# Attention of a two-layer trunk: softplus from a bounded score, and sums over later keys by two f32r products each

## The reference, cut to what matters

```
z = einsum('bhqd,bhkd->bhqk', q, k)                 # q already scaled
visible = arange(nk) < start + arange(nq)           # strictly causal
log_keep = where(visible, log_sigmoid(-z), 0)       # = -softplus(z)
later = cumsum(log_keep, reverse over keys) - log_keep
w = where(visible, exp(log_sigmoid(z) + later), 0)
out = einsum('bhqk,bhkd->bhqd', w, v)
```

## Time and profile before

| | |
|---|---|
| median of three runs | 1333.18 us |
| the profiled execution, own time | 1332.71 us |
| its span | 1331.0 us |
| TensorE busy | 1285.5 us (97%) |
| VectorE busy | 808.4 us (61%) |
| ScalarE busy | 640.2 us (48%) |
| GpSimd busy | 328.2 us (25%) |

### The profile page before, as it was taken

The page is one execution under the profiler, slowest core; times in us unless marked ns, Lnnn a source line. Parts: engine busy times, 40 slices in busy tenths (PEclk is TensorE's granted clock), DMA queues, the critical chain, the costliest instruction groups (busy, mean ns, idle before and its releaser), DMA issues.

```text
span 1331.0 us, 23141 instructions
## 1 busy us (share of the span) xinstructions
PE 1285.5 (97%) x9758; PEld 1173.9 (88%) x9758; DVE 808.4 (61%) x1357; ACT 640.2 (48%) x989; POOL 328.2 (25%) x183
## 2 busy tenths in 40 slices
PE   7999998999999999999999999999999999999996
PEld 6999855999999999999998988877787898998984
DVE  6989654466667375483656456365557673745745
ACT  4344587455346245263564335364354462552634
POOL 0001154265110201102654124114652102011040
PEclk9999999999999999999999999999999999999997
DMA  6641100222233223223222112112322333232311
GB/s 190 150 101 34 66 1 1 83 77 85 76 94 118 77 92 122 77 93 123 65 68 67 59 63 65 64 64 95 95 64 95 96 104 101 92 116 95 99 60 64
DMA packets 112151, 111.49 MB, mean 84 GB/s; under 512 B 8144, under 2 KB 109728, under 8 KB 112048
## 3 DMA queue, kind: packets, MB, share of 16 engines
q1 hardware_dynamic: 108528, 106.77, 25.0%
q0 software_dynamic: 3120, 3.15, 1.5%
q10 hardware_dynamic: 400, 0.11, 0.0%
HBM read 107.91 MB, written 2.10 MB: 83 GB/s over the span
## 4 chain that ended last, share of the span: by engine, by line
PE 79%; DVE 9%; ACT 7%; issue 2%; DMA 2%; POOL 1%; DVEq 0%; SPq 0%; ACTq 0%
PE pb L827 41%; PE pb L1037 6%; PE pb L1039 6%; PE pb L1038 6%; PE pb L998 2%; PE pb L999 2%; PE pb L1000 2%; PE pb L839 1%; PE pb L938 1%; PE pb L939 1%; PE pb L937 1%; ACT wh L1502 1%; PE pb L1279 1%; DVE wl L2164 1%; PE pb L876 1%
## 5 line engine op out<-in xcount | busy, mean ns | idle before, releaser
L676 POOL TENSOR_TENSOR wl<-raw,wh 128x2048 fp32r<-128x2048 f32 x40 | 185.3, 4633 | 690.0 <-ACT wh L1502 690.0
L827 PE MATMUL pb<-hidh,wh 128*128 128x264 f32 (+1 forms) x744 | 197.4, 319 | 0.2 <-DVE wl L2164 0.2
L827 PE MATMUL pb<-hidl,wh 128*128 128x264 f32 (+1 forms) x744 | 197.4, 320 | 0.0
L827 PE MATMUL pb<-hidh,wl 128*128 128x264 f32 (+1 forms) x744 | 197.3, 319 | 0.0
L1502 ACT ACTIVATE wh<-raw 128x2048 fp32r<-128x2048 f32 x73 | 139.3, 1908 | 95.9 <-DMA raw<-in_mlp_w_down 61.0
L827 PE MATMUL pb<-hh,wh 128*128 128x264 f32 (+1 forms) x584 | 150.0, 318 | 4.9 <-DVE qd L2803 1.6
L827 PE MATMUL pb<-hl,wh 128*128 128x264 f32 (+1 forms) x584 | 145.0, 310 | 0.0
L827 PE MATMUL pb<-hh,wl 128*128 128x264 f32 (+1 forms) x584 | 145.0, 309 | 0.0
L827 PEld LDWEIGHTS pb<-hidh,wh 128*128 128x128 f32 x744 | 123.7, 188 | 10.3 <-DVE wl L2164 0.6
L827 PEld LDWEIGHTS pb<-hidh,wl 128*128 128x128 f32 x744 | 123.4, 188 | 9.7
L827 PEld LDWEIGHTS pb<-hidl,wh 128*128 128x128 f32 x744 | 123.4, 188 | 9.5
(11 more groups left out here) (476 smaller groups left out, 3259.6 us busy)
## 6 DMA issues: line engine op xcount, KB each, us to landing
raw<-in_mlp_w_up SPq DMA_DIRECT2D x32, 1024.0 KB, 5.3
raw<-in_mlp_w_down SPq DMA_DIRECT2D x32, 1024.0 KB, 5.1
raw<-in_w_in_c SPq DMA_DIRECT2D x16, 1024.0 KB, 5.3
raw<-in_w_in_ab SPq DMA_DIRECT2D x8, 1024.0 KB, 7.1
raw<-in_w_out_ab SPq DMA_DIRECT2D x4, 1024.0 KB, 5.1
raw<-in_w_out_c SPq DMA_DIRECT2D x4, 1024.0 KB, 5.1
wl<-in_w_in_ab POOLq DMA_DIRECT2D x3, 1024.0 KB, 11.6
x_tok<-in_x SPq DMA_DIRECT2D x2, 1024.0 KB, 8.3
```

What stands on the lines that cost most here:

```text
L676: pool.tensor_tensor(wl[:, c % RING, :], raw[:, c % RING, :], wh[:, c % RING, :].bitcast(F32), ALU.subtract).then_inc(w_lo, 1)
L827: mm = pe.matmul(pb[:, bank + b, 0:z_ - a], lhs, rhs[:, a:z_], start=first and hi and k == 0, stop=last and k == len(todo) - 1)
```

## The change

`z` is cut at `Z_MAX` = 60 by VectorE into `al` (`bound`), ScalarE takes Exp and Ln of it, without Abs, and VectorE takes max(z, ln(1 + exp(min(z, 60)))) (`soft`). ScalarE copies the result to f32r (`high_part`), VectorE subtracts (`split`). The sums over later keys are made from the two parts by f32r products (`sph`, `spl`) with f32r copies of `ntri` and `nones`; `later_a`, `later_b` and their buffers go, and each piece is multiplied on its own. `sp` shares its memory with `spl` and has eight rows, used by `sp_row`. On VectorE `bound(g+2)` stands between `soft(g)` and `split(g)`; on ScalarE `high_part(g)` stands behind `weigh(g-2)`. `softplus_0` and `acc0` stay as they were.

```
+Z_MAX = 60.0
...
         m0b = ExitStack()
-        sp = sb("sp", [P, 6, 512], F32, m0b)
+        al = sb("al", [P, 2, 512], F32, m0b)
+        w_att = sb("w_att", [P, 4, 512], F32, m0b)
         ntri = sb("ntri", [P, P], F32, m0b)
         nones = sb("nones", [P, P], F32, m0b)
         hide = sb("hide", [P, UNIT_A], F32, m0b)
@@ -240,12 +242,15 @@
         ident_r = sb("ident_r", [P, P], F32R, m0b)
         hide_r = sb("hide_r", [P, UNIT_A], F32R, m0b)
         hide0_r = sb("hide0_r", [P, 4 * NMETA], F32R, m0b)
-        al = sb("al", [P, 2, 512], F32, m0b)
+        ntri_r = sb("ntri_r", [P, P], F32R, m0b)
+        nones_r = sb("nones_r", [P, P], F32R, m0b)
         sp0 = sb("sp0", [P, 2, 4 * NMETA], F32, m0b)
         w0 = sb("w0", [P, 2, 4 * NMETA], F32, m0b)
-        lb = sb("lb", [P, 2, 144], F32, m0b)
-        lc = sb("lc", [P, 2, 272], F32, m0b)
-        w_att = sb("w_att", [P, 4, 512], F32, m0b)
+        sp_home = ExitStack()
+        sp = sb("sp", [P, 8, 512], F32, sp_home)
+        sp_home.close()
+        spl = sb("spl", [P, 8, 512], F32R, m0b)
+        sph = sb("sph", [P, 8, 512], F32R, m0b)
         m0b.close()
...
+        def sp_row(g):
+
+            return 6 + g % 2 if g % 6 < 2 and g // 6 % 2 else g % 6
...
             pe.wait_ge(att_consts, 10)
-            pe.wait_ge(mask_r, 3)
+            pe.wait_ge(mask_r, 5)
...
             def acc(g):
 
                 i, n, s, hd, ps = head(g)
-                sa, sb_ = sp[:, hd, :], sp[:, 2 + hd, :]
-                pe.wait_ge(sp_ready, g + 1)
-
-                def later(c0, c1, x_, stop):
-                    return pe.matmul(pb[:, ZB[n], c0:c1], nones[:, :], x_, start=False, stop=stop, skip_group_check=True)
-
-                pe.matmul(pb[:, ZB[n], 0:UNIT[s]], ntri[:, :], sp[:, n, 0:UNIT[s]], start=False, stop=False, skip_group_check=True)
+                a, b = sp_row(6 * i + hd), sp_row(6 * i + 2 + hd)
+                pe.wait_ge(sp_low, g + 1)
+
+                def later(c0, c1, row, x0, stop=False):
+                    for x_ in (sph, spl):
+                        mm = pe.matmul(pb[:, ZB[n], c0:c1], nones_r[:, :], x_[:, row, x0:x0 + c1 - c0], start=False,
+                                       stop=stop and x_ is spl, skip_group_check=True)
+                    return mm
+
+                for x_ in (sph, spl):
+                    pe.matmul(pb[:, ZB[n], 0:UNIT[s]], ntri_r[:, :], x_[:, sp_row(g), 0:UNIT[s]], start=False, stop=False,
+                              skip_group_check=True)
                 if s == 0:
-                    later(144, 160, sa[:, 0:16], False)
-                    later(416, 432, sa[:, 0:16], False)
-                    mm = later(288, 432, sa[:, 16:160], True)
+                    later(144, 160, a, 0)
+                    later(416, 432, a, 0)
+                    mm = later(288, 432, a, 16, True)
                 elif s == 1:
-                    later(128, 256, sa[:, 160:288], False)
-                    pe.wait_ge(later_ready, 4 * i + hd + 1)
-                    mm = later(256, 400, lb[:, hd, :], True)
+                    later(128, 256, a, 160)
+                    later(256, 400, a, 288)
+                    later(384, 400, a, 0)
+                    mm = later(256, 400, a, 16, True)
                 else:
-                    later(112, 240, sb_[:, 0:P], False)
-                    pe.wait_ge(later_ready, 4 * i + hd + 3)
-                    mm = later(240, 512, lc[:, hd, :], True)
+                    later(112, 240, b, 0)
+                    later(240, 512, b, 128)
+                    later(240, 368, a, 160)
+                    later(368, 512, a, 288)
+                    later(496, 512, a, 0)
+                    mm = later(368, 512, a, 16, True)
                 mm.then_inc(acc_ready, 1)
 
...
+            act.activation(ntri_r[:, :], ntri[:, :], ACT.Copy).then_inc(mask_r, 1)
+            act.activation(nones_r[:, :], nones[:, :], ACT.Copy).then_inc(mask_r, 1)
...
                 n = g % 6
                 c = UNIT[n // 2]
-                act.wait_ge(z_ready, g + 1)
-                if g >= 2:
-                    act.wait_ge(sp_ready, g - 1)
-                softplus_part(al[:, g % 2, 0:c], pb[:, ZB[n], 0:c]).then_inc(l_ready, 1)
+                a = al[:, g % 2, 0:c]
+                act.wait_ge(z_bounded, g + 1)
+                me.step(act.activation(a, a, ACT.Exp))
+                me.settle()
+                act.activation(a, a, ACT.Ln, bias=1.0).then_inc(l_ready, 1)
+
+            def high_part(g):
+
+                r, c = sp_row(g), UNIT[g % 6 // 2]
+                act.wait_ge(sp_ready, g + 1)
+                act.activation(sph[:, r, 0:c], sp[:, r, 0:c], ACT.Copy).then_inc(sp_high, 1)
 
...
                 pre(g)
                 if g >= 2:
                     weigh(g - 2)
+                high_part(g)
...
+            def bound(g):
+
+                n = g % 6
+                c = UNIT[n // 2]
+                dve.wait_ge(z_ready, g + 1)
+                if g >= 2:
+                    dve.wait_ge(sp_ready, g - 1)
+                TS(al[:, g % 2, 0:c], pb[:, ZB[n], 0:c], Z_MAX, None, ALU.min).then_inc(z_bounded, 1)
+
             def soft(g):
 
                 n = g % 6
@@ -2371,23 +2410,14 @@
                 dve.wait_ge(l_ready, g + 1)
                 if g >= 6:
                     dve.wait_ge(acc_ready, g - 3)
-                STT(sp[:, n, 0:c], pb[:, ZB[n], 0:c], 0.0, al[:, g % 2, 0:c], ALU.max, ALU.add).then_inc(sp_ready, 1)
-
-            def later_a(g, hd):
-
-                a, o = sp[:, hd, :], lb[:, hd, :]
-                dve.wait_ge(sp_ready, g + 1)
-                me.step(TT(o, a[:, 288:432], a[:, 16:160], ALU.add))
-                me.settle()
-                TT(o[:, P:144], o[:, P:144], a[:, 0:16], ALU.add).then_inc(later_ready, 1)
-
-            def later_b(g, i, hd):
-
-                a, b, o = sp[:, hd, :], sp[:, 2 + hd, :], lc[:, hd, :]
-                dve.wait_ge(sp_ready, g + 1)
-                dve.wait_ge(later_ready, 4 * i + hd + 1)
-                me.step(TT(o[:, 0:P], b[:, P:256], a[:, 160:288], ALU.add))
-                TT(o[:, P:272], b[:, 256:400], lb[:, hd, :], ALU.add).then_inc(later_ready, 1)
+                TT(sp[:, sp_row(g), 0:c], pb[:, ZB[n], 0:c], al[:, g % 2, 0:c], ALU.max).then_inc(sp_ready, 1)
+
+            def split(g):
+
+                n, r = g % 6, sp_row(g)
+                c = UNIT[n // 2]
+                dve.wait_ge(sp_high, g + 1)
+                TT(spl[:, r, 0:c], sp[:, r, 0:c], sph[:, r, 0:c].bitcast(F32), ALU.subtract).then_inc(sp_low, 1)
 
...
+            bound(0)
+            bound(1)
             for g in range(NUNIT):
                 i, n = divmod(g, 6)
                 s, hd = divmod(n, 2)
                 soft(g)
-                if s == 0:
-                    later_a(g, hd)
-                if s == 1:
-                    later_b(g, i, hd)
+                if g + 2 < NUNIT:
+                    bound(g + 2)
+                split(g)
...
```

More of the change, by code:

```diff
@@ L470, in trunk @@
         z_ready = sem("z_ready")
+        z_bounded = sem("z_bounded")
         l_ready = sem("l_ready")
         sp_ready = sem("sp_ready")
-        later_ready = sem("later_ready")
+        sp_high = sem("sp_high")
+        sp_low = sem("sp_low")
         acc_ready = sem("acc_ready")
```

## The result

| | before | after |
|---|---|---|
| median of 4 runs, us | 1333.72 (1332.52 to 1335.26) | 1390.78 (1385.97 to 1392.81) |
| profiled execution, own time / span | 1332.7 / 1331.0 | 1392.1 / 1390.3 |
| end of the attention in the trace | 226.5 | 284.1 |
| from there to the end | 1104.5 | 1106.2 |

The ratio is 1.042, interval 1.040 to 1.044. The attention takes 57.6 us more, everything behind it 1.7 more. The direction and the mechanism of the queue are as predicted, the size is not: 57 us instead of 19, outside the range of 1340 to 1363.

The account below looks back on a forecast made before the run. A three-engine loop in the attention, whose longest path sets the time, was taken to bound the kernel: 80.8 us against 65.7, so 1332.7 + 15.1 + 4 for collisions = 1351.8, 1352 us; range 1340 to 1363.

Parts of the forecast that it names:

- The loop through VectorE's queue: Attention: minimum(g+2) waits for scores and holds up subtraction and next maximum; loops of 6.4 to 6.9 us, stage +15.1 us.
- a quarter piece of `low`: Attention, VectorE: four such pieces between subtraction and maximum, units 4, 6, 14, 16, at 0.6 us each, 2.4 in all.
- TensorE's clock: Attention: TensorE pieces priced at 2.4 GHz in the main sum; a fall in clock appeared only in rival C.
- rival C: Attention: gaps in GELU pairs lower TensorE's clock once a period, costing 7 us; with collisions at +6, 1361 us; 14%.
- Sums as f32r products: Attention, TensorE: units take 1.05, 1.26, 1.82 us, narrow products 0.115 each; together 4.1 against 4.2, so no gain.
- Rival B: Attention, TensorE: narrow f32r products run at their column count, about -7 us on eleven loops, no collisions: 1341 us; 14%.
- Collisions with GpSimd: Attention: VectorE subtractions wait for GpSimd's TENSOR_TENSORs; between 0 and +6 us, taken as +4.
- Rival A: Attention: ScalarE decides and the loop hides; -0.5 us a period, -2 in all, 1331 us; 8%.
- Signs: Attention ending near 245, TensorE's busy share about three quarters, second units' sums 6.4 to 7 us apart, minimum and copy waiting.

Follow-up runs that it names:

- the two float32 kernels: The change with each sum one float32 product of the high part, minimum two units ahead (1366.45 us) or one ahead (1353.58 us).
- the filled kernel: The change plus unread float32 products of 256 columns, three after the scores and two between a pair's sums, from the fourth pair on: 1364.95 us.
- the float32 kernel: The change with each sum one float32 product of the high part, low part computed but left out, minimum still two ahead: 1366.45 us.
- minimum one ahead and the old sums: The kernel before with only the softplus edit, VectorE's minimum one unit ahead, pre-sums and float32 sums kept: 1329.67 us.
- the change with the minimum one ahead: The change with VectorE taking the minimum of unit g+1 instead of g+2 between maximum and subtraction: 1360.35 us.
- doubled scores: The change with every score product issued twice, the second overwriting the first with the same values: 1394.48 us.

## Why the prediction was wrong in size and right in kind

- **The loop through VectorE's queue: right.** Shown by the minimum's wait (61.8 us, ten loops), by 13 us for one queue position between the two float32 kernels, where I expected 10, and by the paths of 6.7 to 7.3 us in the filled kernel at full clock (forecast 6.4 to 7.1). One there is 9.7: the pair with units 16 and 17, by the prediction's terms 7.1 with a GELU and 0.6 for a quarter piece of `low`, 7.7. The 2.0 more are collisions: a subtraction took 1.75 us instead of 0.69, the quarter piece 1.60 instead of 0.68, both beside GpSimd. Loop and collisions together cost about 19 us: +10.1 on those six paths, 18.5 if the other five were like them. The change itself never ran this loop at full clock.
- **TensorE's clock: the step that failed.** The forecast's sum prices every TensorE piece at 2.4 GHz and has no term for the clock. Only rival C (14%) named it, with the place and the sign, but took a fall to be brief: one per GELU pair, 3.5 us of matmuls at half speed, 7 us in all. Measured are 126 us at 0.50 without a rise, worth about 40 us. I took the one fall of the earlier trace rows (0.57 over 4 us) as the size of every fall; no row bore that out. I should have priced the whole stage at the lower level as the far bound, 1352 + 40 = 1392; measured is 1391. That the low clock takes the f32r sums and the longer loop together is shown by the list of runs, its size by the chain's doubled pieces, and that it is a cause and not a by-product by two kernels that have more work on TensorE and are faster: float32 products for the sums (24 us) and the filling (26 us). Why it does not rise again in the change is not shown. My reading was that the loop holds it down itself, since its TensorE pieces double at half clock and VectorE and ScalarE take no longer; the filled kernel, where the clock stays up, fits this. But the recorded busy share does not: it is 89% in the change at 0.50, and 81% in the float32 kernel at 1.00.
- **Sums as f32r products: nearly right.** At full clock the change's first unit, of 432 columns, takes 154.48 to 155.74 = 1.26 us; one in the filled kernel 238.56 to 239.69 = 1.13, against 1.05. A unit of 400 columns takes 245.36 to 246.68 = 1.32 there against 1.26, and one of 512 229.84 to 231.73 = 1.89 against 1.82. The records of the first unit (TensorE, in order of time):

```profile
154.48 0.46 PE L1294 MATMUL pb<-sph,ntri_r 128*128 128x432 f32 x1
154.78 0.36 PE L1294 MATMUL pb<-spl,ntri_r 128*128 128x432 f32 x1
154.98 0.17 PE L1289 MATMUL pb<-sph,nones_r 128*128 128x16 f32 x1
```

  0.20 from the low part's start to the next is columns / 2.4 GHz (0.18) nearly; the first product has 0.30. The six narrow ones take 154.98 to 155.74, 0.127 each, and 0.62 in the filled kernel's chain, 0.103 each; the forecast had 0.115. That the width does not matter is not quite so: in the filled kernel at full clock the starts are on average 0.09 apart for 16 and for 128 columns and 0.13 for 144. Rival B (1341) is dead, and so is the hope that one pass each halves the sums. (Of the passes that the prediction reckons with there, the Trainium skill's page FP8 and Floating Point Precision (TensorE Precision Notes) states the four of float32. That f32r takes one is shown by the 0.20 us for 432 columns.)
- **Collisions with GpSimd: right, in size too.** VectorE and GpSimd in order of time:

```profile
243.37 1.33 DVE L2420 TENSOR_TENSOR spl<-sp,sph 128x512 fp32r<-128x512 f32 x1
```
```profile
242.60 1.56 POOL L793 TENSOR_TENSOR hl<-uqk,hh 128x528 fp32r<-128x528 f32 x1
244.11 1.51 POOL L781 TENSOR_TENSOR tmq<-uqk 128x528 f32<-128x528 f32 x1
```

  All 24 subtractions have a median of 0.61 us and a longest of 1.95. Six are over 0.7 (1.50, 1.13, 1.95, 0.88, 1.33 and 1.14), all of 512 columns, five beside a two-input operation of GpSimd and one (178.82, 1.13 us) beside a one-input one that follows such; together they are 3.8 us above 0.69 each, where the forecast took 4.
- **Rival A (1331, ScalarE decides): wrong for the change,** but near to what happens with the minimum one ahead and the old sums: 1329.67. That ScalarE's lighter load is the reason there is my reading; no run isolates it.
- **Signs.** The attention's end was expected at 245 and is at 284.1; the second units' sums were to be 6.4 to 7 us apart and are 7.8 to 13.2. The minimum and the copy wait where they were to wait. TensorE's busy share was to fall to about three quarters and is 89%, because the half clock fills the gaps. All that follows moved by 1.7 us together. No sign asked for the granted clock over the whole attention, which would have told first.

Open: what starts the first fall, which every kernel with a fall has between 157.8 and 163.0 us; why the clock then stays at 0.50 in the change; why the change with the minimum one ahead rises and falls four times; and why doubled scores bring 27 us of the clock back while five filling products a pair bring back 88. Not tested: the two f32r products with the pre-sums kept, which would have had fewer narrow products, with copy and subtraction still in the loop.

## What to carry to other kernels

When an edit thins TensorE's work in a loop that also waits for other engines, work out the stage at both levels of the clock: the lower one about doubled its matmuls here and lasted for the whole stage, 126 us. Put an instruction whose input another engine still has to make behind everything others need from that queue; one place in VectorE's order was 13 us here at nearly full clock and 30 with the clock. And count narrow products, not columns: at 0.10 to 0.13 us each, the halved passes were given back. Whether pre-sums on VectorE would have kept the gain was not run.

## What the runs showed of the hardware that I had not expected

TensorE's clock stayed at 0.50 for 126 us while its records cover 89% of the time, was at 0.50 with records over 10.00 of 10.00 us, and stayed at 1.00 over 74 us with records over 81%. With products added that nobody reads it rose to 1.00, stayed there, and the kernel was 26 us faster. An f32r product of 432 columns is followed by the next after 0.30 us when first and 0.20 when second in a pair.
